# A hybrid decoder layer on one core: order and tile shape of small products, spread statistics over all rows, places of the last query weights

## What is computed

```python
n = rmsnorm(h, mix_norm_gain); proj = n @ w_in
q, k = rope(rmsnorm(q)), rope(rmsnorm(k))             # 8 heads of 64; statistic per head and token
y_att = attention over the 64 keys that an indexer picks
# RWKV-7 time mixing, 8 heads of 64: state 64x64 per head, worked in 4 chunks of 64 tokens
state = state * w_t + sa * b_t + v_t * k_t;  y = state @ r_t
y_mem = cross attention into 256 memory tokens        # 4 heads of 128, q and k normed per head
h = h + merged @ w_out
q = rmsnorm(h) @ w_q                                  # 8 heads, 2048 columns
expert = top 16 of the sums of two top 16 lists, per head and token
h = h + sum(gate * gelu(x . u[expert]) * v[expert])   # 256*8*16 rows of u and of v, gathered
```

## Time and profile before

| | us |
|---|---|
| median of 3 runs | 1138.88 (1138.14 to 1146.81) |
| the profiled execution | 1145.0 |
| its span, first to last instruction | 1143.2 |
| TensorE busy, DVE busy, ACT busy | 898.6, 651.1, 392.8 |
| mean granted TensorE clock | 0.840 |

### The profile page before, as it was taken

The page is one execution under the profiler, slowest core; times in us unless marked ns, Lnnn a source line. Parts: engine busy times, 40 slices in busy tenths (PEclk is TensorE's granted clock), DMA queues, the critical chain, the costliest instruction groups (busy, mean ns, idle before and its releaser), DMA issues.

```text
span 1143.2 us, 16309 instructions
## 1 busy us (share of the span) xinstructions
PE 898.6 (79%) x5664; PEld 523.4 (46%) x5664; DVE 651.1 (57%) x1548; ACT 392.8 (34%) x1094; POOL 327.4 (29%) x294
## 2 busy tenths in 40 slices
PE   7999999999999999998767556556566666666566
PEld 6887878778878878874421111111111111111111
DVE  2452532195416242464776776678668767766774
ACT  2025133314312010224543443444344344434443
POOL 0000000021003000024445445434554554455451
PEclk9999989999989999999996777876765776666656
DMA  7443323213212225588999999999999999999996
GB/s 293 147 148 111 123 98 111 91 57 112 75 38 75 75 73 208 199 335 348 426 425 426 428 427 427 428 427 428 427 426 427 426 427 428 428 427 427 427 429 273
DMA packets 46578, 329.54 MB, mean 288 GB/s; under 512 B 5312, under 2 KB 5568, under 8 KB 6976
## 3 DMA queue, kind: packets, MB, share of 16 engines
q0 software_dynamic: 36864, 268.45, 55.8%
q1 hardware_dynamic: 9104, 58.69, 14.8%
q10 hardware_dynamic: 560, 1.70, 0.4%
HBM read 327.78 MB, written 1.05 MB: 288 GB/s over the span
## 4 chain that ended last, share of the span: by engine, by line
PE 49%; DMA 27%; DVE 10%; ACT 6%; issue 6%; POOL 1%; POOLq 0%; DVEq 0%; ACTq 0%
DMA pool_mem<-in_experts,pool_mem 26%; PE psum_proj L610 21%; PE psum_job L982 7%; PE psum_proj L623 5%; DVE pool_mem L1763 4%; PE psum_proj L950 3%; PE psum_job L833 2%; POOL pool_mem L1829 1%; ACT L1257 1%; DVE pool_mem L1704 1%; ACT pool_mem L1264 1%; PE psum_job L639 1%; ACT pool_mem L1261 1%; PE psum_job L659 1%; PE psum_job L645 1%
## 5 line engine op out<-in xcount | busy, mean ns | idle before, releaser
L982 PE MATMUL psum_job<-pool_mem 64*64 64x512 f32 x2048 | 375.5, 845 | 218.6 <-ACT pool_mem L1264 218.2
L1829 POOL DMA_INDIRECT pool_mem<-in_experts,pool_mem x256 | 304.3, 1189 | 441.0 <-PE psum_job L982 277.8
L1763 DVE CUSTOM_DVE_ANT_0 pool_mem<-pool_mem 128x1024 f32<-128x1024 f32 x256 | 310.0, 1225 | 183.0 <-DMA pool_mem<-in_experts,pool_mem 181.9
L982 PEld LDWEIGHTS psum_job<-pool_mem 64*64 64x64 f32 x2048 | 85.3, 171 | 503.8 <-issue 503.5
L610 PE MATMUL psum_proj<-pool_mem 128*128 128x256 f32 x1120 | 252.2, 385 | 0.0
L610 PEld LDWEIGHTS psum_proj<-pool_mem 128*128 128x128 f32 x1120 | 213.9, 193 | 35.2 <-issue 6.0
L1257 ACT ACTIVATE pool_mem<-pool_mem 128x1 f32<-128x1 f32 x256 | 51.6, 202 | 283.1 <-DVE pool_mem L1763 282.6
L1812 POOL TENSOR_TENSOR pool_mem<-pool_mem,const 128x256 f32<-128x256 f32 x24 | 17.5, 751 | 354.0 <-DVE pool_mem L1567 292.4
L1264 ACT ACTIVATE pool_mem<-const,pool_mem 128x64 f32<-128x64 f32 x256 | 89.0, 348 | 26.5 <-PE psum_job L982 0.6
L1261 ACT ACTIVATE pool_mem<-pool_mem 128x1 f32<-128x1 f32 x256 | 75.4, 294 | 9.3
L623 PE MATMUL psum_proj<-pool_mem 128*128 128x256 f32 x256 | 56.3, 380 | 1.6 <-DVE pool_mem L1647 1.6
(11 more groups left out here) (251 smaller groups left out, 771.2 us busy)
## 6 DMA issues: line engine op xcount, KB each, us to landing
pool_mem<-in_weights SPq DMA_DIRECT2D x51, 1024.0 KB, 4.8
pool_mem<-in_experts,pool_mem POOLq DMA_INDIRECT x256, 13.6
pool_mem<-in_xT SPq DMA_DIRECT2D x1, 1024.0 KB, 4.8
pool_mem<-in_memT SPq DMA_DIRECT2D x1, 1024.0 KB, 10.5
pool_mem<-in_x ACTq DMA_DIRECT2D x1, 1024.0 KB, 7.7
const<-in_const SPq DMA_DIRECT2D x1, 820.0 KB, 13.9
rows<-in_rows SPq DMA_DIRECT2D x1, 512.0 KB, 16.1
pool_mem<-in_ffn_gain ACTq DMA_DIRECT2D x1, 512.0 KB, 8.2
```

The costliest lines, as they stand in the source:

```text
L982: ins = mm(sum_bank(t, d)[sum_strip(i, d), :], lhsT=diag[rows_, g % DIAGS, :], rhs=slot[g % SLOTS][rows_, D + 512 * d:D + 512 * d + 512], ...
L1763: ins = V.tensor_tensor_reduce(u, u, xn_tok[:, t, :], 1.0, 0.0, ALU.mult, ALU.add, hid[:, par, s_:s_ + 1])
L1829: G_.indirect_dma_start(slot[s_ % SLOTS], None, t_in["experts"], bass.IndirectOffsetOnAxis(ap=expert_i[:, par, s_:s_ + 1], axis=0)).then_i ...
```

## The change

Per-head sums are written to all 128 rows (the pick matrices become 128 columns wide; each statistic stands in 16 or 32 equal rows), and `spread` reads all 128 rows. The constants grow from 1640 to 2067 columns. Thirteen products of ones run on PE before the first sum. `wl`/`al`, `il` and `as` alternate between row halves; `apv` becomes 64 columns wide and alternates between column halves, both heads landing in one 128x256 result that one copy takes out. In `rhs` and `Y` the products that need neither state nor U come first, then those with the state, then those with U. `S` is 16 products of 64x64 instead of 8 of 64x128, and DVE scales the state once `Y` is done, before it waits for `S`. Query block 6 gets a place of its own and is loaded when the merge is done; block 7 is loaded after query unit 0; the table of keys moves.

```diff
-    out["pick_pairs"][:, 6:8] = p[:, None] // HD == np.arange(2)[None, :]
+    out["pick_pairs"][:, 96:128] = p[:, None] // HD == np.arange(32)[None, :] // 16
+    out["pick_ones"][:, 96:128] = 1.0
+    out["to_heads"] = p[:, None] == 16 * (np.arange(W)[None, :] // HD)
...
-        keysT = part(T0 + 18 * K1, 2, KEYS)
-        spare = [part(Y0, KT, 256), part(Q0, KT, 256), part(T0, KT, 256)]
+        keysT = part(E0 + 3 * K1, 2, KEYS)
+        spare = [part(Y0, KT, 256), part(Q0, KT, 256), part(T0, KT, 256), part(T0 + 16 * K1, KT, 256)]
...
+            load_query(6, sg["merged_ok"], 4)
             load_query(5, proj_full, FIRST_UNIT["out"] + 4)
...
-            for i in (6, 7):
-                load_query(i, proj_full, FIRST_UNIT["peer_q"] + i - 5)
+            load_query(7, proj_full, FIRST_UNIT["peer_q"] + 1)
...
-                        first = n - w - w * k
-                        ins = mm(o[0:n, :], lhsT=pick[:, first:first + n], rhs=sq[:, k, :], start=(k == 0), stop=(k == CT - 1))
+                        first = 96 - 32 * k
+                        ins = mm(o, lhsT=pick[:, first:first + P], rhs=sq[:, k, :], start=(k == 0), stop=(k == CT - 1))
...
             pe.wait_ge(sg["ones_ok"], 1)
+            for _ in range(13):
+                mm(psum_job[:, BANKS - 1, 0:P], lhsT=ones[:, :], rhs=ones[:, :], start=True, stop=True)
             pe.wait_ge(sg["ssq"], 2)
...
+            for i in range(2):
+                o_w, o_a = halves(begin(("wl", i))), halves(begin(("al", i)))
+                for m in range(2):
+                    cols = slice((2 * i + m) * P, (2 * i + m + 1) * P)
+                    ins_w = mm(o_w[:, m, :], lhsT=lora[low, cols], rhs=w_tanh, start=True, stop=True)
+                    ins_a = mm(o_a[:, m, :], lhsT=lora[high, cols], rhs=mixed[high, 12, :], start=True, stop=True)
...
+                for t in range(TILES):
+                    for kt in range(TILES):
+                        for m in range(2):
+                            h = 2 * hp + m
+                            ins = mm(o[HD * m:HD * m + HD, t * P:(t + 1) * P], lhsT=v_tok[:, kt, h * HD:(h + 1) * HD],
                                      rhs=probT[:, 2 * (hp % 2) + m, t, kt, :], start=(kt == 0), stop=(kt == TILES - 1))
...
                 o = begin(("rhs", n))
+                for h in range(HEADS):
+                    hs = slice(h * HD, (h + 1) * HD)
+                    ins = mm(o[tl, hs], lhsT=gram[tl, h, 2, :], rhs=vtok[tl, t, hs], start=(h == 0), stop=(n == 0), ...)
                 if n > 0:
                     wait_read(pe, ("S", n - 1))
+                    ins = from_state(o, 0, tl, tc, True)
...
+                for h in range(HEADS):
+                    mm(o[tl, hs], lhsT=gram[tl, h, 3, :], rhs=vtok[tl, t, hs], ...)
+                if n > 0:
+                    from_state(o, 1, tl, tc, False)
+                wait_read(pe, ("U", n))
+                for h in range(HEADS):
+                    ins = mm(o[tl, hs], lhsT=gram[tl, h, 1, :], rhs=U[tl, hs], start=False, stop=True, ...)
                 end(ins, ("Y", n))
...
+                    for last, src, with_ in ((False, ktok[:, t], vtok[:, t]), (True, btok[:, t], U)):
+                        for h in range(HEADS):
+                            hs, r = slice(h * HD, (h + 1) * HD), slice(HD * (h % 2), HD * (h % 2) + HD)
+                            ins = mm(o[r, (h // 2) * HD:(h // 2 + 1) * HD], lhsT=src[tl, hs], rhs=with_[tl, hs], ...)
...
-                st(V.tensor_copy(y_att[0:64, hp, :], o[0:64, 0, :]))
-                job_read(V.tensor_copy(y_att[64:128, hp, :], o[64:128, 1, :]), ("apv", hp))
+                job_read(V.tensor_copy(y_att[:, hp, :], bank(("apv", hp))[:, 0:S]), ("apv", hp))
...
-                wait_job(dve, ("S", n))
+                wait_job(dve, ("Y", n))
                 for r in halves_:
                     st(V.tensor_tensor(state[r, :, r], state[r, :, r], pe_n[r].to_broadcast([HD, CT, HD]), ALU.mult))
                 st.wait()
+                wait_job(dve, ("S", n))
```

More of the change, by code:

```diff
@@ L184, in job_plan @@
     jobs = [("x_ss",), ("mem_ss",), ("mk_ss",)]
-    jobs += [("wl", i) for i in range(2)] + [("al", i) for i in range(2)]
+    jobs += [(j, i) for i in range(2) for j in ("wl", "al")]
     jobs += [("vt", t) for t in range(TILES)]
@@ L680, in _ @@
             pe.wait_ge(sg["lora_in"], 1)
[L681 to L687, removed]
+            low, high = slice(0, 64), slice(64, 128)
+            for i in range(2):
[4 more added lines that the diff above has]
+                    ins_a = mm(o_a[:, m, :], lhsT=lora[high, cols], rhs=mixed[high, 12, :], start=True, stop=True)
+                end(ins_w, ("wl", i))
+                end(ins_a, ("al", i))
             pe.wait_ge(sg["mixed_ok"], 7)
@@ L732, in _ @@
             for t in range(TILES):
[L733 to L736, removed]
+                o = [halves(begin(("il", t, i))) for i in range(2)]
+                for m in range(2):
+                    for i in range(2):
+                        ins = mm(o[i][:, m, :], lhsT=iqT[64 * i:64 * i + 64, m, t * P:(t + 1) * P],
                                  rhs=ikT[64 * i:64 * i + 64, :], start=True, stop=True)
-                    end(ins, ("il", t, i))
+                        if m == 1:
+                            end(ins, ("il", t, i))
             pe.wait_ge(sg["ends_ok"], 3)
@@ L802, in attention_pair @@
                     attention_scores(hp + 2)
-                o = halves(begin(("apv", hp)))
+                o = begin(("apv", hp))
                 wait_read(pe, ("apt", hp, 0))
@@ L877, in chunk_rhs, with from_state @@
                 o = begin(("rhs", n))
+                for h in range(HEADS):
+                    hs = slice(h * HD, (h + 1) * HD)
+                    ins = mm(o[tl, hs], lhsT=gram[tl, h, 2, :], rhs=vtok[tl, t, hs], start=(h == 0), stop=(n == 0),
+                             skip_group_check=True)
                 if n > 0:
                     wait_read(pe, ("S", n - 1))
+                    ins = from_state(o, 0, tl, tc, True)
+                end(ins, ("rhs", n))
+            def from_state(o, i, tl, tc, last):
                 for cc in range(CT):
[L881 to L887, removed]
+                    ins = mm(o[tl, cc * P:(cc + 1) * P], lhsT=ar[:, cc, i, tc], rhs=state[:, cc, :], start=False, stop=last,
+                             skip_group_check=True)
+                return ins
             def chunk_u(n):
@@ L917, in chunk_y @@
                     o = begin(("S", n))
-                    for cc in range(CT):
-                        cols = slice(cc * P, (cc + 1) * P)
-                        mm(o[:, cols], lhsT=btok[tl, t, cols], rhs=U[tl, cols], start=True, stop=False)
-                        ins = mm(o[:, cols], lhsT=ktok[tl, t, cols], rhs=vtok[tl, t, cols], start=False, stop=True)
+                    for last, src, with_ in ((False, ktok[:, t], vtok[:, t]), (True, btok[:, t], U)):
+                        for h in range(HEADS):
+                            hs, r = slice(h * HD, (h + 1) * HD), slice(HD * (h % 2), HD * (h % 2) + HD)
+                            ins = mm(o[r, (h // 2) * HD:(h // 2 + 1) * HD], lhsT=src[tl, hs], rhs=with_[tl, hs],
+                                     start=(not last and h < 2), stop=last, skip_group_check=True)
                     end(ins, ("S", n))
```

65 lines of the change are left out of this document (26 added, 39 removed).

## The result

The changed kernel takes 1126.03 us (median of 4 runs, 1124.62 to 1128.02). The kernel before took 1141.47 us beside it (4 runs, 1138.14 to 1146.81). The ratio is 0.986, with a 95% interval of 0.983 to 0.989. The profiled execution of after took 1125.06 us, its span is 1123.2 us, and its mean granted clock is 0.848. Of all executions reported here one was slow, 1664.6 us in the kernel with `pool_mem` at byte 17408, and it is left out of that kernel's median and ratio.

What follows compares the result with a forecast made beforehand. PE's work ahead of the first gather was taken to bound the kernel, with the gather's length fixed. Terms summed to 23.3 us; 16.8 plus half of the other 6.5, taken as 20 from the median 1138.9, gave 1119 us, range 1111 to 1128.

Steps and rivals of the forecast that it cites:

- The step that failed: Last stage: the gather's length is its bytes over 425 GB/s, and no edit touches it.
- lead products: Start of PE, ahead of L639: thirteen products of ones bring full clock, gain 3.05 us, bounds 0 and 3.05.
- full rows and first clock stretch: Spreads of `mk` and `mq` at L659: full rows gain 0.4 us, the half clock behind them goes, 3.4 us.
- second clock stretch: Half clock behind the second spreads of L659, at 232.6 to 236.0 us: goes with full rows, 1.4 us taken.
- third clock stretch: Half clock in the first chunk, 317.9 to 324.7 us: bounds 0 and 3.4 us, 1.7 taken.
- The rival (the clock falls again in the gap): Ahead of L639: lead products don't help, 3 us less gain, 1122 us; chance 0.12.
- Column halves at 128 rows: `apv`, four times: alternating column halves run together, 2.04 to 1.04 us each, gain 4.0 us, bounds 0 and 4.0.
- the rival of 4 us: `apv`: column halves at 128 rows don't run together, 4 us less gain, 1123 us; chance 0.12.
- Small blocks: Chunks: `rhs` to 2.3 us, `Y` to 3.4, `S` to 1.08; gains 2.1, 2.6 and 2.7 us in all.
- Waits in place of work: Pairs and chunks: half of 12.4 us gain lost to waits for ACT and DVE, 6 us, 1125 us; chance 0.10.
- Slower through the clock: Chunks and pairs, 308 to 418 us: PE stays at half clock, up to 110 us more, 1229 us; chance 0.06.
- The median: Whole kernel: 1138.9 us, 6.1 below the profiled execution; so only half of the 6.5 us of stretch terms counted.

Runs made afterwards that it cites:

- The shifted kernel: Kernel before with its on-chip constants table allocated 2067 columns wide (1640 used), so `pool_mem` starts at byte 37568: 1151.97 us, ratio 1.009.
- the aligned ones: Changed kernel with `pool_mem` moved to byte 17408 by declaration order, or to 37632 by a table 2088 columns wide: 1117.87 and 1119.20 us.
- second profile of before: Kernel before, unchanged, profiled once more: 1138.5 us, first gather at 485.10 us.
- second profile of after: Changed kernel, unchanged, run and profiled again: 1126.72 us, ratio 0.987 to the kernel before.
- unaligned variants: Changed kernel with constants padded in DRAM, or on-chip table 2072 or 2120 columns wide: 1124.78, 1127.26, 1125.30 us.

## Why the forecast went as it did

The direction and the size came out: 1126.0 lies in the range of 1111 to 1128, and is 15.4 us or 1.4% below the kernel before beside it. The likeliest value, 1119, was 7 us too low. That 1126.0 still lies in the range is in part luck: no bound of the range had a slower gather in it, and a front that gave more than the sum made up for half of that loss. The total hides one step that failed and some terms of a wrong size.

**The step that failed.** "The last stage is the gather: its length is its bytes over that rate, and no edit touches it." The first half holds: the DMA share is 1.01 to the end in every kernel, and each time follows from the rate. The second half is wrong. The prediction counted the 427 new constant columns as bytes to be loaded ("half a microsecond at 425 GB/s") and did not ask what lies behind the table in on-chip memory. The rate fell from 427 to 422 GB/s, 6.4 us. The prediction had named the sign of it, "a gather stage longer by what the front lost", but as a matter of overlap and not of the rate. The shifted kernel makes the loss in before, and the aligned ones remove it from after. With that, after takes 1117.9 to 1119.2 us, the forecast's value. That agreement is in part luck, for two errors cancel in it: the forecast took 20 us from a median of 1138.9, and these kernels are 24 to 26 us below a median of 1143.5.

**The terms of the sum**, by the two profiles:

| step | forecast | measured | |
|---|---|---|---|
| lead products | 3.05 | 3.0 | L639 6.67 to 3.72; L639's start and the rest equal |
| `wl`, `al` | 0.8 | 0.3 | 1.0 won, 0.70 of it into a wait for ACT at 98.09 |
| `as`, `il` | 0 | 0 | 1.07 to 1.06; 3.00 to 3.02 |
| full rows and first clock stretch | 3.8 | 3.6 | 15.28 to 11.65 us for the same work from L659 |
| second clock stretch | 1.5 | 1.3 | 6.37 to 5.05 us |
| pairs 0 and 1 (two `apv`, copies) | 2.0 + 0.6 | 2.1 | 5.71 to 4.72 and 4.46 to 3.38 us; `apv` 2.04 to 1.09 |
| chunk 0 with its gate and `apv` | | 6.0 | 21.3 to 15.3 us |
| chunks 1, 2, 3 | | 4.8, 3.0, 1.95 | 17.57 to 12.81, 13.77 to 10.77, 11.80 to 9.85 |
| in these: `rhs` | 0.7 a chunk | 0.85 a chunk | 2.94 to 2.09 |
| in these: `Y` | 0.7 a chunk | 1.14 a chunk | 4.11 to 2.97 |
| in these: `S` | 0.9 a chunk | 1.04 a chunk | 1.98 to 0.94 |
| in these: third clock stretch | 1.7 | 3.4 | none in the profile of after |
| pairs and chunks together | 14.1 | 17.9 | |
| block 7 | 0 | 0.0 | 25.24 us to the ninth gather in both |

The 14.1 are the forecast's terms of `apv` and its copies, `rhs`, `Y`, `S`, the wait of L826 and the third stretch. The measured rows make 26.1 of the 26.7 us; the rest lies in small shifts between them. Of the 3.4 us over the sum of 23.3, 1.7 is the third stretch and most of the rest the small blocks.

*Lead products.* Right in the wait and in the gain. Their own length was not: 6.6 us was forecast, in order to match the 6.7 us after which L639 had turned fast, and it was 4.80 to 5.92 us in the nine profiles, eight of which had the whole gain. The rival (the clock falls again in the gap) had 0.12, and one profile of nine showed it, in part.

*Full rows.* Right: both stretches went, and the kernel with them alone and the one without them show that it is this edit. That a wider operation costs ACT and DVE nothing held too (1739 ns a reciprocal, 1728).

*Column halves at 128 rows.* The Trainium skill (TensorE: Matmul & The Clock Gate, Part 3: Packing small matmuls) has weight loads overlap with products in flight only where the row group differs. Here all 128 rows are in use in each of the 16 instructions of L819, only the columns alternate, and they take 1.09 us, 0.068 each, where full products of the same length take 0.128. So the trace doesn't agree with the rule for this case, and the rival of 4 us fell. The extension of the earlier trace rows from 64 rows to 128 was sound. The copies' 0.6 was not: of the 2.1 us of pairs 0 and 1, the two `apv` make 1.9. In pair 0 the 96 instructions behind `apv` take 3.69 us before and 3.63 after, from the first start to that of L610; the second copy is gone, and PE stands there for 0.47 us without a releaser that the profile names.

*Small blocks.* For `rhs` 2.3 was forecast and 2.09 measured, for `Y` 3.4 and 2.97, for `S` 1.08 and 0.94. All three were somewhat too long; the products with the state run at 1.02 us for eight, as estimated, and the changes of shape cost next to nothing once there are few of them.

*The third stretch.* I took the half, and it went wholly in the profile of after: 1.7 us more than forecast. Why it went is open. In the kernel with full rows alone it was there, 10.2 us long, and none of the eight profiles with the new order has one between 240 and 400 us, which speaks for the denser order within pairs and chunks. But of the six profiles with the old order three have none there either (the second profile of before, the lead products alone, before shifted), so its absence can also be chance. No run takes the order apart. A later stretch, of 3.4 us near 401 us, is in two of the eight: the second profile of after and the one with the table 2072 columns wide, with their first gathers at 466.16 and 466.36 us in place of 464.58.

*Waits in place of work* had 0.10, for half of the gain of pairs and chunks. New waits of 0.70 and 0.82 us stand outside of the pairs and chunks; the 0.47 us within pair 0 stands in place of shorter ones of before. The 0.41 us wait of L826 for DVE is gone, as forecast, and the chunks gave more than their terms, so that rival fell.

*Slower through the clock* fell: no half clock stretch stands between 240 and 420 us in the profile of after, and one of 3.4 us in its second profile.

*The median.* "Half clock stretches are what an execution can have fewer of" was right, and the second profile of before shows it: one stretch in place of three, with the first gather 6.2 us earlier. The three runs shown gave a low median for before: with more runs it is 1142 to 1144. Against that, after and its unaligned variants won 15 to 19 us, and the aligned ones with full rows 24 to 26.

## What to carry to other kernels

A buffer that gathers of rows like these (8 KB) write to should start at a multiple of 256 bytes in each partition, and in a kernel laid out like this one its place is fixed by every table declared ahead of it: an edit to a table's width is an edit to the rate of the last stage, and a full DMA share does not show that rate falling, only the GB/s beside it do. Products that use a few rows of the array for some microseconds can cost nearly as much again through the clock behind them (4.0 us of `mk` and `mq`, then 3.4 us for 6.8 us at half clock); writing the statistics to all rows cost no time here and kept the clock. Two small products on different halves of the columns run together also at 128 rows, so a product of which half is thrown away is worth splitting.

## What was not expected of the hardware

- Gathers of 8192-byte rows took 309 ns a packet (median and 95%) to slots that start at a multiple of 256 bytes, and 312 (95%: 319 to 321) to slots at 192 or 128 bytes past one: 427 against 422 GB/s, some 6 us of 1120. All else in `pool_mem` moved with the slots; that the slots are what counts is argued from the packets, which write there. The 8 KB packets of the weight blocks, which SP issues into the same `pool_mem`, have a median of 309 ns before and after; why only the gather shows it is open. The Trainium skill (DMA: Bandwidth & Descriptors, How a descriptor splits into AXI transactions) tells of a boundary at 256 bytes: a transfer that doesn't start there begins at the boundary below and moves bytes that it doesn't need. It says so of what is read. Here the edit that made the loss in before moved only the written side, and the runs agree with the 256, so the written side shows such a boundary too; the padded tables in DRAM grew by multiples of 256 bytes alone (427 and 85 columns of 512 bytes), so what the read side does is not shown.
- PE was at half clock behind products that had kept it busy, with 4 or 8 rows in use (and the kernels with few rows), and at full clock through the same work with 128 rows: 3.4 to 6.8 us at 0.50 to 0.55 against a clock of 1.00 for 453 us.
- In one profile of nine the clock was at 0.50 for L639, behind 4.80 us of lead products and 1.83 us of idle PE; in the next nearest, 4.96 and 1.72 us, L639 ran at full pace.
- Alternating column halves at 128 rows: 0.068 us for an instruction of 128 columns, against 0.128 without.
